# One input projection scheme for every column group: products with tokens as rows, turned by VectorE through DRAM

## What is computed

```
h = RMSNorm(x)                                  # 256 x 2048
u = h @ W_in                                    # 2048 x 5664, columns q k v f | x B C z dt
y_fox = attention of 16 heads with cumulative forget terms, per-frame causal
xBC = silu(causal_dwconv4(x, B, C))             # conv along the tokens
y = chunked state-space scan(xBC, dt) + D * x
y_ssd = RMSNorm(y * silu(z)) * norm_w
x = x + concat(y_fox, y_ssd) @ W_out            # 2048 x 2048
```

## Time and profile before

| | us |
|---|---|
| median of 3 runs | 1210.68 |
| the profiled execution, whole | 1210.89 |
| its span on the core | 1209.2 |
| TensorE busy in the span | 1197.4 |
| VectorE busy | 809.1 |
| ScalarE busy | 669.9 |
| POOL busy | 48.1 |

### The profile page before, as it was taken

One profiled execution on the slowest core, in us unless ns is written; L12 is line 12 of the kernel. 1 busy time (PEld: TensorE's weight loads), 2 busy tenths in 40 slices (PEclk: granted clock), 3 DMA queues, 4 the chain that ended last, 5 costly groups with the idle time before them and its releaser, 6 DMA issues.

```text
span 1209.2 us, 17387 instructions
## 1 busy us (share of the span) xinstructions
PE 1197.4 (99%) x5800; PEld 1005.5 (83%) x5800; DVE 809.1 (67%) x1194; ACT 669.9 (55%) x899; POOL 48.1 (4%) x69
## 2 busy tenths in 40 slices
PE   9999999999999999999999999999999999999997
PEld 7888888888888788888888888888888888888886
DVE  5698787788876576676766767667655555545555
ACT  6455786775555555555645655555444444445555
POOL 3200220002100000000000000000000000000000
PEclk9999999999999999999999999999999999999999
DMA  9566886445688778878788787787767676767663
GB/s 284 170 181 180 245 242 184 127 123 174 214 240 263 240 228 247 246 238 249 228 246 245 237 245 230 248 248 228 237 218 215 208 208 216 215 207 248 204 194 105
DMA packets 225497, 263.13 MB, mean 218 GB/s; under 512 B 13840, under 2 KB 168676, under 8 KB 225316
## 3 DMA queue, kind: packets, MB, share of 16 engines
q1 hardware_dynamic: 223444, 257.13, 70.1%
q0 software_dynamic: 1824, 5.04, 1.5%
q10 hardware_dynamic: 176, 0.27, 0.1%
HBM read 242.94 MB, written 17.87 MB: 216 GB/s over the span
## 4 chain that ended last, share of the span: by engine, by line
PE 97%; ACT 1%; DMA 1%; DVE 1%; SPq 0%; issue 0%; ACTq 0%
PE ps L1063 13%; PE ps L1065 13%; PE ps L1064 13%; PE ps L395 10%; PE ps L1099 7%; PE ps L1100 7%; PE ps L1098 7%; PE ps L466 6%; PE ps L468 6%; PE ps L467 6%; PE ps L393 5%; PE ps L369 2%; PE ps L993 1%; DMA turned_cols<-turn_dram 0%; PE ps L1008 0%; PE ps L973 0%
## 5 line engine op out<-in xcount | busy, mean ns | idle before, releaser
L358 DVE TENSOR_TENSOR w_lo<-w_raw,w_hi 128x1024 fp32r<-128x1024 f32 x412 | 506.2, 1233 | 335.0 <-ACT w_hi L353 333.9
L353 ACT ACTIVATE w_hi<-w_raw 128x1024 fp32r<-128x1024 f32 x412 | 434.6, 1058 | 418.9 <-PE ps L1065 205.6
L1063 PE MATMUL ps<-w_hi,h_parts 128*128 128x512 f32 x704 | 274.0, 389 | 1.2 <-DVE h_parts L1490 1.2
L1065 PE MATMUL ps<-w_hi,h_parts 128*128 128x512 f32 x704 | 273.9, 389 | 0.0
L1064 PE MATMUL ps<-w_lo,h_parts 128*128 128x512 f32 x704 | 273.9, 389 | 0.0
L395 PE MATMUL ps<-h_parts,w_hi 128*128 128x512 f32 x512 | 180.6, 395 | 0.0
L1063 PEld LDWEIGHTS ps<-w_hi,h_parts 128*128 128x128 f32 x704 | 132.1, 188 | 28.9 <-DVE h_parts L1490 1.6
L1065 PEld LDWEIGHTS ps<-w_hi,h_parts 128*128 128x128 f32 x704 | 132.1, 188 | 27.6
L1064 PEld LDWEIGHTS ps<-w_lo,h_parts 128*128 128x128 f32 x704 | 132.1, 188 | 27.3
L393 PE MATMUL ps<-h_parts,w_lo 128*128 128x256 f32 x512 | 145.8, 285 | 0.0
L1098 PE MATMUL ps<-w_hi,act_parts 128*128 128x512 f32 x352 | 136.9, 389 | 0.0
(11 more groups left out here) (268 smaller groups left out, 1176.1 us busy)
## 6 DMA issues: line engine op xcount, KB each, us to landing
w_raw<-in_w_gate_up SPq DMA_DIRECT2D x352, 256.0 KB, 3.6
w_raw<-in_w_down SPq DMA_DIRECT2D x88, 512.0 KB, 4.7
w_raw<-in_w_in SPq DMA_DIRECT2D x87, 512.0 KB, 4.1
w_raw<-in_w_out SPq DMA_DIRECT2D x32, 512.0 KB, 4.6
w_raw<-in_w_ple_gate SPq DMA_DIRECT2D x32, 512.0 KB, 4.7
unit_cols<-unit_dram SPq DMA_DIRECT2D x88, 128.0 KB, 3.1
unit_dram<-rms SPq DMA_DIRECT2D x22, 256.0 KB, 3.2
unit_dram<-unit_spare SPq DMA_DIRECT2D x22, 256.0 KB, 3.5
```

What stands on the lines that cost most here:

```text
L353: act.activation(parts(n)[0], w_raw[:, n % RING, :], ACT.Copy).then_inc(w_hi_made, 1)
L358: dve.tensor_tensor(lo, w_raw[:, n % RING, :], hi, ALU.subtract).then_inc(w_lo_made, 1)
L1063: pe.matmul(dst, a, hi, start=first and kk == 0, stop=False)
L1065: mm = pe.matmul(dst, b, hi, start=False, stop=last and kk == 1)
```

## The change

All 11 groups of the input projection now have tokens as rows, with 12 matmuls of 512 columns a chunk. The order of groups is bc, x0, x1, k0, q0, k1, q1, v0, v1, z0, z1. The first group (bc) still runs in passes, but with 512 columns (12 a chunk). Every group but v leaves in one way (`leave_group`): ScalarE copies both 128 x 512 halves with the token's root as scale, VectorE turns 32 x 32 blocks, SyncE writes them to `group_dram` and reads them back as channels into `group_cols` (for the convolution), `kE`/`kO`, `qE`/`qO` or `zT`. The queries are read in 16 pieces with runs of 128 bytes (32 numbers), all others in 4 with runs of 512 bytes. Keys and z keep the blocked layout: a tile's 256 tokens stand in 8 runs of 32. `spread_rms`, `copy_rms`, `take_part`, `leave_q0` and POOL's `ferry` go. Tiles are placed so that every matmul operand starts at a multiple of 128 bytes; before, `pHi`, `pLo`, `sumsq` and `prob` did not.

```diff
-CONV_STEPS = 7
+CONV_STEPS = 12
-    halves = [(g, 0, KP // 2) for g in range(3)] + [(g, KP // 2, KP) for g in range(3)] + [(3, 0, KP)]
+    halves = [(g, a, a + KP // 2) for a in (0, KP // 2) for g in range(D // COLS)]
+        def multiply_by_pass(pe, n, kks, banks, last, hi_made, lo_made, turn=None):
+            def one_pass(parts_, h_part):
+                for kk in kks:
+                    for t in range(TT):
+                        mm = pe.matmul(ps[:, banks[t], :], h_part[:, k, t * P:(t + 1) * P],
+                                       parts_[:, n % RING, kk * COLS:(kk + 1) * COLS], ...)
+        def group_to_dram(sp, name):
+            for t, blocks in enumerate((first_blocks[:, :], group_spare(i))):
+                sp.wait_ge(group_turned, TT * i + t + 1)
+                if t == 0 and i > 0:
+                    sp.wait_ge(*group_landings(turned_names[i - 1]))
+                sp.dma_start(group_dram[t], blocks).then_inc(group_out, 16)
+        def group_from_dram(sp, name):
+            sp.wait_ge(group_out, 16 * TT * (i + 1))
+            if name in conv_names and i > 0:
+                sp.wait_ge(conv_step, 2 * CONV_STEPS * i)
+            if name[0] == "z":
+                sp.wait_ge(mix_lo_made, WT // 4 * (int(name[1]) + 1))
...
+        GROUP_OUT, GROUP_BACK, GROUP_READY, Z0_LATER = LEAD + 5, LEAD + 6, LEAD + 6, 3
+                    after(sp_before, n + GROUP_OUT, "group_to_dram", g.name)
...
-            all_after(end["z1"] + 6, "gate_norm")
+            all_after(end["z1"] + 11, "gate_norm")
-                n = end["z1"] + 7 + b + LEAD
+                n = end["z1"] + 12 + b + LEAD
                 after(dve_after, n, "scale_ssd", b)
...
                     if g.name == "o3":
-                        pe.wait_ge(mix_lo_made, WT)
+                        pe.wait_ge(prob_lo_made, H)
+                        pe.wait_ge(y_root_made, 1)
...
+            def leave_group(g):                                   # ScalarE
+                for t in range(TT):
+                    copy(unit_tok[:, t, :], ps[:, g.banks[t], :], scale[:, t:t + 1]).then_inc(group_left, 1)
+            def square_z(half):                                   # ScalarE
+                act.wait_ge(gated, 2 * half + 2)
+                act.activation(y_squares[half][...], xsT[:, MT * half:MT * (half + 1), :], ACT.Square).then_inc(z_squared, 1)
...
+            def conv_taps(u, back):                               # VectorE
+                for over in range(2):
+                    for e in range(2):
+                        dst, src = by_block(conv_out[:, u % 2, e, :]), group_cols[:, :, 2 * (u % 2) + e, :]
+                        if over:
+                            dst, src = dst[:, 1:, 0:back], src[:, :TT * NB - 1, BLK - back:]
+                        else:
+                            dst, src = dst[:, :, back:], src[:, :, :BLK - back]
```

More of the change, by code:

```diff
@@ L382, in multiply_by_pass @@
             pe.wait_ge(*lo_made)
[L383 to L401 removed]
+            return one_pass(w_lo, hHi)
         UNIT_BANKS = (SET_C, SET_A)
@@ L455, in multiply_group @@
             first, last = c == 0, c == g.chunks - 1
-            if g.wide:
-                return multiply_wide(pe, n, lambda k: h_parts[:, 4 * c + k, :, :], g.banks, first, last)
             pe.wait_ge(w_lo_made, n + 1)
@@ L554, in plan @@
-            all_after(end["q0"] + 10, "cums")
-            after(dve_after, end["q0"] + 11 + LEAD, "make_row", 0)
-            after(dve_after, end["q0"] + 12 + LEAD, "make_row", 1)
-            all_after(end["bc"] + 10, "cb", 0)
-            all_after(end["bc"] + 13, "cb", 1)
-            all_after(end["x0"] + 7, "turn_xs", 0)
-            all_after(end["x1"] + 7, "turn_xs", 1)
-            b0 = end["x1"] + 9
+                n = end[g.name]
+                step = "leave_v" if g.name[0] == "v" else "leave_group"
@@ new lines, in plan @@
+                after(act_after, n + LEAD, step, g)
+                after(dve_after, n + LEAD, step, g)
+                if g.name[0] != "v":
+                    after(sp_before, n + GROUP_OUT, "group_to_dram", g.name)
+                    if g.name[0] == "q":
+                        for b in range(2):
+                            after(sp_before, n + GROUP_BACK + 2 * b, "queries_from_dram", g.name, (2 * b, 2 * b + 1))
+                    else:
+                        late = Z0_LATER if g.name == "z0" else 0
+                        after(sp_before, n + GROUP_BACK + late, "group_from_dram", g.name)
@@ new lines, in plan @@
+                if g.name in conv_names:
+                    for b in range(2):
+                        u = 2 * conv_names.index(g.name) + b
+                        m = n + GROUP_READY + b * KC - b
+                        after(act_after, m, "conv_first", u)
+                        for back in range(1, KC):
+                            after(dve_after, m + back - 1, "conv_taps", u, back)
+                        after(act_after, m + KC - 1, "conv_silu", u)
+            all_after(e0 + 1, "turn_par")
@@ new lines, in plan @@
+            after(pe_after, e0 + 2, "fd")
+            after(dve_after, e0 + 2 + LEAD, "fd")
+            after(act_after, e0 + 5 + LEAD, "fd")
+            after(pe_after, e0 + 4, "turn_fd")
+            after(dve_after, e0 + 4 + LEAD, "logits")
+            after(dve_after, e0 + 6 + LEAD, "softplus")
+            after(pe_after, e0 + 8, "turn_falls")
+            after(dve_after, e0 + 8 + LEAD, "cumulate")
+            all_after(e0 + 10, "cums")
+            after(dve_after, e0 + 11 + LEAD, "make_row", 0)
@@ L563, in plan @@
+            after(dve_after, e0 + 12 + LEAD, "make_row", 1)
+            all_after(e0 + 14, "cb", 0)
+            all_after(e0 + 16, "cb", 1)
+            all_after(end["x0"] + 13, "turn_xs", 0)
+            all_after(end["x1"] + 13, "turn_xs", 1)
+            b0 = end["x1"] + 17
             for i in range(H + 2):
@@ L1518, in invert_root @@
                 dve.wait_ge(root_made, norm + 1)
[L1519 to L1526 removed]
+                dve.reciprocal(rms_col[:, :], root[:, :]).then_inc(rms_col_made, 1)
@@ L1792, in turn_par @@
                 ins.then_inc(par_copied, 1)
-            steps = dict(leave_q0=leave_q0, take_part=take_part, turn_par=turn_par, stats0=stats0, fd=fd, logits=logits, softplus=softplus,
+            steps = dict(leave_group=leave_group, turn_par=turn_par, turn_p=p_lo, fd=fd, logits=logits, softplus=softplus,
                          cumulate=cumulate, make_row=make_row,
```

399 lines of the change are left out of this document (157 added, 242 removed).

## The result

The changed kernel takes 1214.01 us (median of 8 runs, 1213.27 to 1215.27) against 1210.49 us (8 runs, 1210.04 to 1211.43): ratio 1.0029, 95% interval 1.0018 to 1.0039. It is slower by 0.3%; 1208.0 was forecast, and 1214.0 lies above the range that ended at 1213.5. The profiled execution spans 1212.1 us against 1209.2.

What follows compares the result with a forecast made beforehand. TensorE, busy in 1197.4 of 1209.2 us, bounds the kernel; only matmul start distances or new waits count. Against 1210.9: -6.35 and +3.7 make -2.65, so 1208.2, less 0.2 for the median: 1208.0 us, range 1204.0 to 1213.5.

Steps and rivals of the forecast that it cites:

- the -0.3 us of `pHi` and `pLo`: TensorE: all 48 matmuls with pHi or pLo gain 7 ns each once their tiles are aligned, -0.3 us.
- The hand-over of o3: Last group of W_out into feed-forward: o3's read back waits for o2's h, starting later, all on the path, +3.0 us.
- the rival "the hand-over doesn't grow": End of W_out: o3's hand-over costs nothing more, giving 1205.0 us; chance 0.18.
- The prediction's other lock, the write-out: Ahead of o3's read back: the write-out also waits for o2's landing; both locks open at about the same time.
- Projection, first group, root: Input projection: faster token-form chunks -4.7 us, first group in long matmuls -0.9, spreading the root dropped -0.45.
- 4.45: Chunks 8 to 87: predicted gain in us from projection, root and cumulative sums together.
- Cumulative sums: Convolution stage: TensorE's wait for VectorE's scan cum grows, +0.7 us, from 0 to 2.2.
- Covered items: DRAM turning, query reads and POOL's squares moved to ScalarE: hidden behind TensorE, 0 us each.
- the rival of the lagging VectorE: Convolution stage, slots 16 to 29: TensorE waits for w_lo and turn_xs, 1215.5 us; chance 0.2 together with gapped keys.
- its rival at 5.0: Query reads in runs of 128 bytes stall the load ring, two stalls of 2.5 us, 1213.0 us; chance 0.06.
- The score products with gapped keys: Attention: score matmuls reading keys in gapped 128-byte runs cost 0; from above a doubling, 10 us.
- I am wrong if that wait stays near 1 us: Sign against the forecast: TensorE's wait for o3's h behind chunk 125, predicted at some 4 us, stays near 1.

Runs made afterwards that it cites:

- e1: Changed kernel with its arena (mixHi, mixLo, act_parts, last_hi and the other tiles placed by hand) 128 bytes higher: 1205.72 us, ratio 0.9966.
- e2: Kernel before, with par_mix and x_ssq allocated ahead of h_parts, so weights and h stand 128 bytes higher, arena unmoved: 1218.92 us, ratio 1.0068.
- e6: Changed kernel with an unused 128-byte tile ahead of xtok and its arena 128 bytes above that again, all operands at 0 modulo 256: 1205.35 us.
- e4: Kernel before with only the new order of W_out's chunks (first halves of o0 to o3, then second halves): 1212.87 us, ratio 1.0019.
- e5: Changed kernel with its arena 64 bytes higher: 1208.85 us, ratio 0.9988.
- e3: Changed kernel with one unused 128-byte tile ahead of xtok, so all tiles stand 128 bytes higher: 1213.37 us, ratio 1.0030.
- m2: Products only, without the kernel's computation, for equal, unequal and alternating address pairs: equal 226.7 ns, unequal 232.5; bf16 215.8 ns a product.

## Why the prediction was wrong, step by step

**Placement, the step that failed.** The prediction has the -0.3 us of `pHi` and `pLo`, read from 396 ns against 389 for "those with aligned tiles" as a matter of alignment to 128 bytes, and it follows only the tiles that the change speaks of. Its rows were right and their cause was wrong: 396 ns was the price of a difference, and that price is paid by all of W_out and W_down once the arena lands on another remainder. It measured +2.36 and +6.03 us, with nothing of it in the sum. e1 removes it, e2 makes it without the change. Even the -0.3 holds in part only: the 36 products of `pHi` and `pLo` with `w_hi` and `w_lo` fell from 396 to 389 ns, the 12 with `last_hi` and `last_lo`, in the arena, stayed at 393 to 395, so that the -0.35 of the last part is luck in part. With the term of placement the forecast is 1208.0 + 8.4 = 1216.4 us, and with the next one as measured, 3.55 less, 1212.9; the result is 1214.0. The two misses have opposite signs: without the cost of placement (e1, e6) the kernel lies some 2.5 us below the forecast, inside the range.

**The hand-over of o3: +3.0 predicted, -0.55 measured.** SyncE's timeline in the kernel before:

```profile
389.15 1.20 SPq L332 DMA_DIRECT2D w_raw<-in_w_gate_up  x2
```

SyncE's and then VectorE's in the changed one:

```profile
386.91 2.58 SPq L325 DMA_DIRECT2D w_raw<-in_w_gate_up  x2
391.22 1.79 SPq L468 DMA_DIRECT2D turned_cols<-turn_dram  x4
```

```profile
396.06 1.67 DVE L1486 SCALAR_TENSOR_TENSOR h_parts<-turned_cols,par,h_parts 128x256 fp32r<-128x256 f32 x4
```

391.22 - 379.93 = 11.29 us behind the start of chunk 120, 3.01 later than before: the lock works as the prediction says. What failed is that the transfer was taken to be as slow as today. From issue to h it takes 4.84 us instead of 8.44, and the last loads ahead of it end their issue 1.73 us earlier (386.91 + 2.58), no longer 0.10 us (389.15 + 1.20 against 390.45). One execution doesn't settle this term, though. The other traces have the same hand-over (us; the start of the read back is counted from the start of chunk 120):

| kernel | order of W_out | read back starts | from its issue to h | TensorE waits |
|---|---|---|---|---|
| before | old | 8.28 | 8.44 | 1.2 |
| e2 | old | 8.28 | 7.85 | 0.5 |
| e4 | new | 11.24 | 6.45 | 2.1 |
| changed | new | 11.29 | 4.84 | 0.5 |
| e5 | new | 11.23 | 5.29 | 1.0 |
| e3 | new | 11.81 | 4.93 | 1.2 |
| e1 | new | 12.24 | 4.98 | 1.2 |
| e6 | new | 13.00 | 4.89 | 2.3 |

In every trace of the new order the read back starts 3.0 to 4.7 us later and is 1.4 to 3.6 us quicker. The wait varies from one execution to the next by as much as it grew, so -0.55 is one draw: e1, the same kernel with another placement, has +0.54 in these chunks, e6 +2.80. So the rival "the hand-over doesn't grow" was near for the changed kernel, not shown, and the +3.0 was too much for it. Why the read back is quicker stays open. Loads issued longer ahead of it are one candidate, not tested; they can't be all, for in e4 these loads end their issue 3.05 us ahead and it still takes 6.45 us. The prediction's other lock, the write-out, counts too: in e1, e3 and e6 o2's h is made 0.3 to 1.9 us before the read back is issued, and the chain that ended last runs through the write of `turn_dram`, 6.5 to 8.0 us long.

**Projection, first group, root: right.** -4.60 at chunk 88 with 0.40 lost at the start. The first group gave 0.84 for 0.9. Chunks 8 to 87 gave 4.16 for 4.45, with a new wait of 0.5 us for `probT_lo` among them; e1, without that wait, gains 4.61 there. That the 4.45 comes out holds for the sum of its terms; they were not measured one by one. All of TensorE's waits in the changed kernel:

```profile
PE ps L836 <- DVE idle_in L1772: 1.3, 1, 1.3
PE ps L842 <- DMA mix_rows<-in_mix_norm_w: 1.0, 1, 1.0
PE ps L1051 <- DVE h_parts L1486: 0.5, 1, 0.5
PE ps L995 <- DVE probT_lo L1674: 0.5, 1, 0.5
PE ps L362 <- ACT w_hi L346: 0.5, 1, 0.5
```

**Cumulative sums: +0.7 was too much.** They start at 66.88 us, 1.81 earlier than before, and 0.32 us behind the product ahead of them where it was 0.46 before, so no wait has grown there.

**Covered items: right but for the queries.** Beyond the start of the kernel TensorE waits for no `w_lo` and no tap, so the rival of the lagging VectorE falls. The wait of 0.5 us for `probT_lo`, however, leads back to the queries. In the chain that ended last of the changed kernel it hangs on a load that SyncE could issue only behind eight reads of q0 (137.12 to 140.90 us), and that took 6.31 us:

```profile
140.95 6.31 DMA w_raw<-in_w_in
156.66 0.53 DVE probT_lo L1674
```

Between these two stand `w_hi`, `w_lo` and the steps of the attention on ScalarE and VectorE. The prediction had this cost at 0 and its rival at 5.0; it was 0.5 us here and nothing in e1, e3, e5 and e6, the same kernel at other addresses. So that rival falls by its size, not by its mechanism. The score products with gapped keys last as long as before, 380 ns for the larger ones (274 for the smaller, 273 before), and two of them take 0.43 us in the chain as before:

```profile
L980 PE MATMUL ps<-kO,qO 128*128 128x256 f32 x16 | 4.8, 380 | 0.0
```

The prediction's condition "I am wrong if that wait stays near 1 us" came true, but in the kernel's favour; its list of signs had none for products that change their pace outside the projection.

The best version is the changed kernel with its operands on one remainder, 1205.35 (e6) or 1205.72 us (e1). That is what the change is worth, some 5 us against the kernel before; 8.3 us of placement hid it.

## What to carry to other kernels

When a change adds or removes tiles, write down the address of every matmul operand before and after, and look at the remainder of the pair, not at the alignment of each. Where two shapes of one product differ by a few ns without a wait, find out why before using the number, and multiply it by all the products that it could come to hold for. When a transfer starts later, don't carry its old duration over: it took 8.44 us before and 4.84 after. And a wait that differs between executions by as much as the term in question (0.5 to 2.3 us here) is to be read from several traces.

## What was not expected of the hardware

The Trainium skill says under "SBUF — State Buffer" (Operand start alignment) that a start must be a multiple of the element size, and calls this a matter "about legality, not speed". These runs give the speed: 226.7 to 227.3 ns for a product of 512 columns in fp32r on equal remainders, 229 to 234 otherwise, at addresses that are all multiples of 32. The Trainium skill's page "TensorE: Matmul & The Clock Gate" (Back-to-back issue gap) gives N / 2.4 + 2.5 ns as the gap of a matmul by itself, an estimate of 215.8 for 512 columns, with no word on addresses. The bf16 products of m2 take just that, 215.8 ns, those in fp32r about 11 ns more.

A wait can cost more than its length. In e6's profiled execution TensorE stood 2.35 us for o3's h, 0.2 us longer than in e4. The stretches behind it (granted clock third from the end):

```profile
395.80:397.00 1.20, 1.20 (x5) 1.03 (x6) 0.78 (x3) 1.04 (x1) 0.00 (x0) 0.89 0.77 232
397.00:398.00 1.00, 1.00 (x4) 0.71 (x3) 1.00 (x1) 0.00 (x0) 0.00 (x0) 0.50 0.91 283
398.00:399.00 1.00, 1.00 (x4) 0.81 (x3) 0.10 (x1) 0.00 (x0) 0.00 (x0) 0.50 0.96 319
399.00:400.00 1.00, 1.00 (x4) 0.81 (x3) 0.00 (x0) 0.00 (x0) 0.00 (x0) 0.50 1.08 376
400.00:401.00 1.00, 1.00 (x5) 0.76 (x5) 0.00 (x0) 0.60 (x1) 0.00 (x0) 0.93 0.91 277
```

The granted clock falls to 0.50, 1.2 instead of 2.4 GHz, for some 3 us, and that chunk takes 4.43 us where it takes 2.86 in the kernel before: 1.6 us on top of the wait. In e4 the clock stayed at 1.00 after a wait of 2.13 us. It is one execution each. e6's three other runs took 1205.06 to 1205.58 us, the profiled one 1208.04, which fits a hand-over that differs from one execution to the next.
